# Modulation sums by 32x32 transposes and one fold; the second norm's squares added on VectorE

## The chip, the cores and the metric

The kernel runs on one core of one Trainium2 chip. The metric is the device time of one execution in microseconds (us); less is better. The engines are called TensorE (PE; its weight loads are PEld), VectorE (DVE), ScalarE (ACT), GpSimd (POOL) and SyncE (SP, which here only issues DMAs).

## The reference, cut to what matters

One layer of a block over 512 tokens of width 1024, in float32:

```python
c_act = silu(c)                                   # 1024
mod = c_act @ w_ada + b_ada                       # 1024 x 6144: six rows of 1024
shift1, scale1, gate1, shift2, scale2, gate2 = split(mod, 6)
h = rmsnorm(x, norm1_g) * (1 + scale1) + shift1
... projections, sliding-window attention, stick-breaking attention, merge ...
x = x + gate1 * (merged @ w_out)
h2 = rmsnorm(x, norm2_g) * (1 + scale2) + shift2  # needs sum of x*x over the 1024 features
x = x + gate2 * peer(h2, ...)
out = rmsnorm(x, final_g)
```

Two sums matter here. The modulation row `mod` is a sum over 1024 rows of `w_ada`; its first 16 columns of 128 values are needed before the first projection, the other 32 only after the attention. The second norm needs, for each token, the sum of squares of the new `x` over its 1024 features.

## The kernel before, in words

Features lie on the 128 partitions, tokens on the free axis: `x` is 8 chunks (k) of 128 x 512. Matrix products are made of three TensorE passes on split values (high by high, high by low, low by high; `PASSES`), each a matmul of 128x128 weights against 128x512. A weight block (128x1024) is loaded by SP, its high part is copied by ScalarE (`block_high`, L1010), its low part is subtracted by GpSimd (`block_low`, L562), and TensorE runs its 24 matmuls. Two blocks of split weights are in store, so ScalarE starts on block t + 2 when block t is done. Each engine runs its own program in the order of the code; semaphores order the engines against each other.

The modulation. `w_ada` comes in 12 pieces of 512 columns. `ada_product` (L1344, L1346) on VectorE makes, in 8 instructions over 128x512 in SBUF, each waiting for the one before, a 128x512 partial sum `adap` of a piece: its columns still have to be summed over the 128 partitions. `ada_sum` (L643) does that on TensorE: four float32 matmuls with 128 columns of `adap` as weights and one column of ones as the moving side; each float32 matmul shows as two in the trace, so a sum is 8 rows of 128x1. Pieces 0 to 3 are worked before the attention. Pieces 4 to 11 are worked in the eight heads of the attention loop, one in each.

The attention loop goes over heads n = 0 to 7, two heads to a pair. In each head TensorE runs `heads_scores` (L710 to L725), three or four projection blocks of `FILL[n]` (L684) and, ahead of the third, `turn_probs` (L733) and `later_sums` (the 128x1 rows of L643 for n > 0, then L749, L752), then `head_outputs` (L765, L773). Even heads have value and gate blocks; heads 1, 3 and 5 have the next pair's query and key blocks; head 7 has three gate blocks. VectorE goes in each head through the softmax of the window (L1435 to L1444), the stick-breaking terms (L1450, L1453), `keep(0)` (L1431: a copy of a gate block out of PSUM), `ada_product`, `keep(1)`, then in heads 1, 3 and 5 `rope` (L1408 to L1412), then the other `keep`s and the copies of the outputs (L1462, L1464). `rope` reads bank 7, which `head_outputs` overwrites, so TensorE's L765 waits for `rope_ready`. A projection block writes the bank of the block two before it, so in even heads the fourth block waits for `keep(1)`.

After the loop come eight `up` blocks and eight `out` blocks (L843). After each `out` block m VectorE adds to `x` (L1489), ScalarE squares chunk m into one of two buffers (`squares`, L993), and TensorE sums the squares of chunk m - 1 over the partitions after its block m (`rms_sum`, L630, 8 rows of 128x1). At m = 2 and 4 ScalarE also copies the high part of a query weight (L1112, 128x2048) and GpSimd makes its low part (`query_low`, L567), ahead of its next `block_low`. At the end: the sum of chunk 7, the root on ScalarE (L998), its reciprocal on VectorE, the spread over the partitions on TensorE (L637) and the second norm (L1499).

Of the kernel before, what the change touches and what calls it, by code (L numbers as in the profile page):

```python
# [23 lines left out]
HEADS = 8  # L24
# [36 lines left out]
ALU = mybir.AluOpType  # L61
# [7 lines left out]

(K_ID, K_ONE, K_NTRI, K_NONE, K_SBM, K_CAUS, K_ROT, K_IOTA, K_NEVER, K_SWA, K_INV, K_EPS, K_END) = (  # L70
    0, 128, 256, 384, 512, 640, 768, 896, 1024, 1152, 1408, 1409, 1410)

# [98 lines left out]
def build(nc, xT, small, consts, pos, w_ada, w_blocks, w_qry, skT, euT, ev, eu, gf_row, out):  # L171
    with ExitStack() as ctx:
# [124 lines left out]
        assert att_end <= ARENA - 2 * PAIRS * T, att_end  # L297
        squares2 = yB[:, 2:4, :]

# [63 lines left out]
        def a_buffer(i):  # L363
# [10 lines left out]
        ring_free = [sem(f"ring_free{s}") for s in range(4)]  # L374
        ada_ready, ada_summed, ada_direct, ada_row, ada_turned = map(sem, (
            "ada_ready", "ada_summed", "ada_direct", "ada_row", "ada_turned"))
        hi_ready, h_split, u_hi, u_split, v_hi, v_split, a_split = map(sem, (
# [246 lines left out]
        def _(pe):  # L624
# [14 lines left out]
            def ada_sum(n, b, bank, col):  # L639

                pe.wait_ge(ada_ready, n + 1)
                for m in range(4):
                    last = pe.matmul(bank[:, bass.ds(col + m, 1)], adap[:, b, m * P:(m + 1) * P], ones[:, 0:1], start=(n < 3 and m == 0), stop=True, skip_group_check=True)  # L643
                last.then_inc(ada_summed, 1)
# [5 lines left out]
            for k in range(DC):  # L650
# [3 lines left out]
                last = pe.matmul(ps[4][0:1, :], cact[:, k:k + 1], ring[:, 0, k * 512:(k + 1) * 512], start=(k == 0), stop=(k == DC - 1))  # L654
            last.then_inc(ada_direct, 1)
# [3 lines left out]
            last.then_inc(ada_turned, 1)  # L659
            ada_sum(2, 0, ps[6], 12)  # L660
# [155 lines left out]

            ada_sum(HEADS + 2, 0, ps[2], 256 + 4 * (HEADS - 1))
            pe.wait_ge(oa_out, HEADS)
# [3 lines left out]
            for t in range(UNIT0, len(BLOCKS)):  # L822
# [157 lines left out]
        def _(sa):  # L980
# [3 lines left out]
            def squares(first, dst, chunks=range(DC)):  # L984
                for k in chunks:
                    if k == DC - 1:
                        act_(tiny[:], cst[:, K_EPS:K_EPS + 1], ACT.Sqrt)
                    if first:
                        sa.wait_ge(x_ready, first - DC + k + 1)
                    buffers = dst.shape[1]  # L990
                    if k >= buffers:
                        sa.wait_ge(sq_summed, first + k - buffers + 1)
                    act_(dst[:, k % buffers, :], x[:, k, :], ACT.Square).then_inc(sq_ready, 1)  # L993

            def root(n):

                sa.wait_ge(sq_summed, n * DC)
                act_(rms[:], ps[7][:, 0:TT], ACT.Sqrt, scale=1.0 / D, bias=cst[:, K_EPS:K_EPS + 1]).then_inc(root_ready, 1)  # L998
# [47 lines left out]
            block_high(1)  # L1046
            sa.wait_ge(ada_direct, 1)
            act_(arow[0:1, :], ps[4][0:1, :], ACT.Copy).then_inc(ada_row, 1)
# [82 lines left out]
            for t in range(UNIT0, len(BLOCKS)):  # L1131
# [192 lines left out]
        def _(ve):  # L1324
# [13 lines left out]
            def ada_product(n, slot, b, loads):  # L1338

                ve.wait_ge(ring_in[slot], loads * 16)  # L1340
                if n >= 2:
                    ve.wait_ge(ada_summed, n - 1)
                w = ring[:, slot, :].rearrange("p (k n) -> p k n", k=DC)
# [5 lines left out]
                ins.then_inc(ada_ready, 1)  # L1349
                ve.wait_ge(ada_ready, n + 1)  # L1350
                ve.sem_inc(ring_free[slot], 1)


# [67 lines left out]
            for n in range(HEADS):  # L1421
# [327 lines left out]
def constants():  # L1749
# [80 lines left out]
```

## Time and profile before

| | |
|---|---|
| median of 3 runs | 1722.92 us (1720.43 to 1722.98) |
| span of the profiled execution | 1720.5 us |
| TensorE matmul busy | 1687.4 us, 98% of the span |
| VectorE busy | 1357.2 us, 79% |
| ScalarE busy | 717.8 us, 42% |
| GpSimd busy | 642.7 us, 37% |
| chain that ended last | PE 82%, DVE 15%, issue 2%, ACT 1%, DMA 1% |

The span is from the first to the last instruction of one execution; the profile gives no other time for that execution, and the runs are timed apart from it. In a timeline a row is a start and a length in us from the span's start, then engine, line and operation; the bracket is the time the engine had sat idle, and what ended that. PEclk is TensorE's granted clock, 1.00 for 2.4 GHz and 0.50 for 1.2 GHz. A wait for "issue" is one for which the profile shows no releaser. The attention loop lies at about 84 to 350 us, the `up` blocks to 398, the `out` blocks to 448, the second norm and the first query block to 468; two thirds of the span are the expert stage after them.

### The profile page before, as it was taken

To read this page: it belongs to the slowest core of one execution; us is meant where nothing else is said; L and a number is where in the kernel's file an instruction comes from. 1 tells how busy PE (TensorE), PEld (TensorE's weight loads), DVE (VectorE), ACT (ScalarE), POOL (GpSimd) and SP (SyncE) were. 2 spreads that over 40 slices of the span, in tenths; PEclk is the share of its full clock that TensorE was granted. 3 is DMA by queue.
4 is the path that set the end of the run, shared out by engine and by line. 5 is a ranking of instruction groups with operands and counts; after the bars stand their busy time and mean duration, and the time that the engine had idled before them with its cause. 6 is when DMAs were issued, how large, how long until landed. Compare 5 with 4: busy or idle time off the path is not lost.

```text
span 1720.5 us, 24258 instructions
## 1 busy us (share of the span) xinstructions
PE 1687.4 (98%) x8795; PEld 1490.7 (87%) x8795; DVE 1357.2 (79%) x2770; ACT 717.8 (42%) x1119; POOL 642.7 (37%) x372
## 2 busy tenths in 40 slices
PE   6999999999999999999999999999999999999998
PEld 4688777878899999999999999999999988888886
DVE  7447546674589998999999488888878799989897
ACT  3356455543443443444444333333333344333334
POOL 0322222235356674611111055555434454333331
PEclk9999999999999999999999999999999999999999
DMA  8222332433143433567777899999988899999993
GB/s 338 102 98 86 126 156 86 147 119 139 39 138 115 148 126 102 196 213 286 282 267 266 298 373 362 333 355 339 337 315 307 274 386 407 398 386 384 380 385 123
DMA packets 162156, 417.97 MB, mean 243 GB/s; under 512 B 13584, under 2 KB 83216, under 8 KB 156176
## 3 DMA queue, kind: packets, MB, share of 16 engines
q1 hardware_dynamic: 113680, 266.88, 42.8%
q0 software_dynamic: 36864, 134.23, 21.3%
q10 hardware_dynamic: 11520, 15.73, 2.5%
q8 instruction: 46, 0.75, 0.2%
q14 instruction: 46, 0.38, 0.1%
HBM read 373.80 MB, written 42.99 MB: 242 GB/s over the span
## 4 chain that ended last, share of the span: by engine, by line
PE 82%; DVE 15%; issue 2%; ACT 1%; DMA 1%; POOL 0%; SPq 0%; ACTq 0%
PE bank L944 30%; PE bank L897 22%; PE bank L684 10%; PE bank L843 5%; PE bank L932 5%; PE bank L630 1%; PE bank L710 1%; DVE arena L1595 1%; DVE idx L1534 1%; DVE arena L1556 1%; DVE arena L1548 1%; PE bank L773 1%; DVE arena L1549 1%; DVE slots L1527 1%; PE bank L752 1%
## 5 line engine op out<-in xcount | busy, mean ns | idle before, releaser
L897 PE MATMUL bank<-h_split,u_split 128*128 128x384 f32 x3072 | 556.9, 337 | 2.3 <-DVE u_split L1511 2.0
L897 PEld LDWEIGHTS bank<-h_split,u_split 128*128 128x128 f32 x3072 | 534.6, 188 | 8.6 <-DVE u_split L1511 2.3
L944 PE MATMUL bank<-v_late,a_late 128*128 128x512 f32 x1440 | 326.7, 390 | 0.0
L944 PEld LDWEIGHTS bank<-v_late,a_late 128*128 128x128 f32 x1440 | 270.3, 188 | 56.0
L589 POOL DMA_INDIRECT rows<-eu,idx x128 | 181.3, 1416 | 361.3 <-DVE dots L1516 339.4
L589 POOL DMA_INDIRECT rows<-ev,idx x128 | 173.4, 1355 | 244.3 <-DVE row_sum L1622 211.8
L562 POOL TENSOR_TENSOR block_split<-arena,block_split 128x1024 fp32r<-128x1024 f32 x48 | 117.2, 2445 | 310.5 <-ACT block_split L1010 310.5
L1159 ACT ACTIVATE gelus<-bank 128x384 f32<-128x384 f32 x128 | 62.9, 491 | 370.1 <-PE bank L897 370.0
L944 PE MATMUL bank<-v_split,a_split 128*128 128x512 f32 x864 | 205.4, 391 | 0.0
L944 PEld LDWEIGHTS bank<-v_split,a_split 128*128 128x128 f32 x864 | 161.6, 188 | 31.9
L1622 DVE SCALAR_TENSOR_TENSOR row_sum<-rows,agate,row_sum 128x1024 f32<-128x1024 f32 x127 | 162.6, 1280 | 4.4 <-DVE row_sum L1622 0.5
L684 PE MATMUL bank<-h_hi_part,block_split 128*128 128x512 f32 x512 | 160.9, 396 | 0.5 <-POOL block_split L562 0.5
L1516 DVE CUSTOM_DVE_ANT_0 rows<-rows,h_rows 128x1024 f32<-128x1024 f32 x128 | 151.3, 1220 | 4.4 <-DMA rows<-eu,idx 4.4
L1259 ACT ACTIVATE v_late<-v_raw 128x1024 fp32r<-128x1024 f32 x80 | 84.8, 1060 | 149.8 <-PE bank L944 149.7
L1511 DVE TENSOR_TENSOR u_split<-u_raw,u_split 128x1024 fp32r<-128x1024 f32 x92 | 114.5, 1245 | 39.8 <-ACT u_split L1150 39.8
L1150 ACT ACTIVATE u_split<-u_raw 128x1024 fp32r<-128x1024 f32 x128 | 134.4, 1051 | 0.0
L572 POOL TENSOR_TENSOR u_split<-u_raw,u_split 128x1024 fp32r<-128x1024 f32 x36 | 87.9, 2450 | 109.1 <-ACT u_split L1150 109.1
L1652 DVE TENSOR_TENSOR v_late<-v_raw,v_late 128x1024 fp32r<-128x1024 f32 x80 | 97.8, 1222 | 24.0 <-ACT v_late L1259 22.0
L684 PEld LDWEIGHTS bank<-h_hi_part,block_split 128*128 128x128 f32 x512 | 95.4, 188 | 21.4 <-POOL block_split L562 1.3
L1664 DVE TENSOR_TENSOR weights<-gelus,gates 128x384 f32<-128x384 f32 x128 | 70.9, 554 | 52.0 <-issue 46.3
L1633 DVE TENSOR_SCALAR hot_j<-cst,slots_turned 128x128 f32<-128x128 f32 x384 | 106.5, 344 | 0.0
L1010 ACT ACTIVATE block_split<-arena 128x1024 fp32r<-128x1024 f32 x50 | 52.8, 1056 | 116.3 <-DMA arena<-w_blocks 56.2
(251 smaller groups left out, 2397.3 us busy)
## 6 DMA issues: line engine op xcount, KB each, us to landing
u_raw<-euT SPq DMA_DIRECT2D x128, 512.0 KB, 6.7
v_raw<-ev SPq DMA_DIRECT2D x128, 512.0 KB, 6.8
arena<-w_blocks SPq DMA_DIRECT2D x50, 512.0 KB, 8.9
arena<-w_ada SPq DMA_DIRECT2D x12, 2048.0 KB, 8.1
gates_scratch<-stage SPq DMA_DIRECT2D x24, 1024.0 KB, 10.7
gates<-gates_scratch SPq DMA_DIRECT2D x64, 384.0 KB, 8.1
gelu_scratch<-gelus ACTq DMA_DIRECT2D x80, 192.0 KB, 3.6
gelus<-gelu_scratch SPq DMA_DIRECT2D x80, 192.0 KB, 8.7
```

Source lines behind the costliest of these rows:

```text
L562: nc.gpsimd.tensor_tensor(ws[:, t % 2, 1, :], wraw[:, t % 4, :], ws[:, t % 2, 0, :].bitcast(F32), ALU.subtract).then_inc(w_split, 1)
L572: nc.gpsimd.tensor_tensor(us[:, c % 2, 1, :], ut[:, c % RING, :], us[:, c % 2, 0, :].bitcast(F32), ALU.subtract).then_inc(u_split, 1)
L589: pool.indirect_dma_start(rows[g % NG], None, eu if g < P else ev_rows, bass.IndirectOffsetOnAxis(ap=idx[:, g % P:g % P + 1], axis=0)).the ...
L684: last = pe.matmul(ps[bank][:], ws[:, t % 2, wp, k * P:(k + 1) * P], h1s[xp][:, k, :], start=(k == 0 and q == 0), stop=(k == DC - 1 and q ...
L897: last = pe.matmul(ps[6 + b][:, 0:TD], us[:, b, wp, k * P:(k + 1) * P], hs[:, xp, k, 0:TD], start=(k == 0 and q == 0), stop=(k == DC - 1 a ...
L944: last = pe.matmul(ps[2 * t + f][:], a[:, ap, t * P:(t + 1) * P], v[:, vp, f * 512:(f + 1) * 512], start=(first and q == 0), stop=True, sk ...
L1150: act_(us[:, c % 2, 0, :], ut[:, c % RING, :], ACT.Copy).then_inc(u_hi, 1)
L1511: nv.tensor_tensor(us[:, c % 2, 1, :], ut[:, c % RING, :], us[:, c % 2, 0, :].bitcast(F32), ALU.subtract).then_inc(u_split, 1)
L1516: nv.tensor_tensor_reduce(rows[k % NG], rows[k % NG], hT, 1.0, 0.0, ALU.mult, ALU.add, dots[:, k:k + 1]).then_inc(rows_used, 1)
L1622: nv.scalar_tensor_tensor(acc, rows[g % NG], agate[:, k:k + 1], acc, ALU.mult, ALU.add).then_inc(rows_used, 1)
L1633: ins = nv.tensor_scalar(ohj[:, b, q, :], cst[:, K_IOTA:K_IOTA + P], slotsT[:, 1, t:t + 1], slotsT[:, 2, t:t + 1], ALU.is_equal, ALU.mult)
L1652: nv.tensor_tensor(v_buffer(i)[:, 1, :], vt[:, i % RING, :], v_buffer(i)[:, 0, :].bitcast(F32), ALU.subtract).then_inc(v_split, 1)
```

## The change

1. In the heads, `ada_sum` is gone. After `keep(1)` VectorE runs `ada_fold(n)`: a transpose of `adap` in blocks of 32x32 (128x512), and a reduction of each block's rows to 128x16 values, kept in `ada_parts` (in the space of `dots`).
2. After the last head TensorE sums what is left over the four groups of 32 partitions: 4 float32 matmuls with 32 moving columns and a constant 0/1 matrix `K_FOLD`.
3. `ada_product` always writes `adap[:, 0]`, and no longer waits for sums on TensorE in the heads.
4. In the `out` stage square 0 goes to `square_sum`, squares 1 to 7 to one buffer `square`. VectorE adds squares 1 to 6 to `square_sum`, the one of chunk m - 1 after its L1489 of block m. ScalarE waits for that addition before square m (m >= 2). TensorE has no sum between the blocks; after the last it sums `square_sum` (after addition 6), then `square` (after square 7).
5. The constants lose an unused 128 columns and gain 224: 1410 columns become 1506.

```diff
@@ TensorE
 def later_sums(n):
-                if n:
-                    ada_sum(n + 2, n % 2, ps[2], 252 + 4 * n)
@@ after the heads
-            ada_sum(HEADS + 2, 0, ps[2], 256 + 4 * (HEADS - 1))
+            pe.wait_ge(ada_ready, 3 + 2 * HEADS)
+            of_32 = ada_parts.rearrange("p n (m b) -> p n m b", m=4)
+            for b in range(4):
+                last = pe.matmul(ps[2][:, 256:288].rearrange("p (n m) -> p n m", n=HEADS), cst[:, K_FOLD + 96 - 32 * b:K_FOLD + 224 - 32 * b],
+                                 of_32[:, :, :, b], start=False, stop=True, skip_group_check=True)
+            last.then_inc(ada_summed, 1)
@@ up and out blocks
-                if kind == "out" and m:
-                    rms_sum(DC, squares2, [m - 1])
-            rms_sum(DC, squares2, [DC - 1])
+            pe.wait_ge(squares_added, DC - 2)
+            for t in range(TT):
+                pe.matmul(ps[7][:, t:t + 1], square_sum[:, t * P:(t + 1) * P], ones[:, 0:1], start=(t == 0), stop=False, skip_group_check=True)
+            pe.wait_ge(sq_ready, 2 * DC)
+            for t in range(TT):
+                last = pe.matmul(ps[7][:, t:t + 1], square[:, t * P:(t + 1) * P], ones[:, 0:1], start=False, stop=True, skip_group_check=True)
+            last.then_inc(sq_summed, 1)
@@ ScalarE, out block m
-                    squares(DC, squares2, [m])
+                    if m == DC - 1:
+                        act_(tiny[:], cst[:, K_EPS:K_EPS + 1], ACT.Sqrt)
+                    sa.wait_ge(x_ready, m + 1)
+                    if m >= 2:
+                        sa.wait_ge(squares_added, m - 1)
+                    act_(square if m else square_sum, x[:, m, :], ACT.Square).then_inc(sq_ready, 1)
@@ VectorE
+            def ada_fold(n):
+                step(nv.transpose(adap[:, 1, :], adap[:, 0, :]))
+                nv.tensor_reduce(ada_parts[:, n, :], adap[:, 1, :].rearrange("p (c r) -> p c r", c=16), AX.X, ALU.add).then_inc(ada_ready, 1)
@@ VectorE, head n
                 keep(0)
-                ada_product(n + 3, 0, (n + 1) % 2, n + 2)
+                ada_product(n + 3, 0, 0, n + 2)
                 keep(1)
+                ada_fold(n)
                 if a == 1 and i + 1 < PAIRS:
                     rope(i + 3, halves)
@@ VectorE, out block m
+            def add_square(m):
+                ve.wait_ge(sq_ready, DC + m + 1)
+                if m >= 2:
+                    ve.wait_ge(squares_added, m - 1)
+                nv.tensor_tensor(square_sum, square_sum, square, ALU.add).then_inc(squares_added, 1)
                     nv.scalar_tensor_tensor(x[:, m, :], ps[m % 2][:], part(2, m), x[:, m, :], ALU.mult, ALU.add).then_inc(x_ready, 1)
+                    if m >= 2:
+                        add_square(m - 1)
```

## Rows read from the trace of the kernel before

**Rows 1.** The page: busy time by engine; the chain by engine.
```profile
PE 1687.4 (98%) x8795; PEld 1490.7 (87%) x8795; DVE 1357.2 (79%) x2770; ACT 717.8 (42%) x1119; POOL 642.7 (37%) x372
PE 82%; DVE 15%; issue 2%; ACT 1%; DMA 1%; POOL 0%; SPq 0%; ACTq 0%
```
**Rows 2.** TensorE's waits: who waited for whom, total, times, longest.
```profile
PE bank L765 <- issue: 2.2, 3, 0.7
```
**Rows 3.** Timeline of TensorE in head 1.
```profile
137.66 0.95 PE L643 MATMUL bank<-cst,arena 128*128 128x1 f32 x8
138.48 0.48 PE L752 MATMUL bank<-sp_hi,from_r 128*128 128x512 f32 x1
...
147.67 1.71 PE L765 MATMUL bank<-arena 128*64 128x128 f32 x14 [0.72 <-issue]
```
**Rows 4.** Timeline of VectorE in head 1.
```profile
134.42 9.48 DVE L1346 SCALAR_TENSOR_TENSOR arena<-arena,cact 128x512 f32<-128x512 f32 x7
144.05 1.39 DVE L1408 TENSOR_TENSOR arena<-arena 64x512 f32<-64x512 f32 x2
...
146.18 1.39 DVE L1412 TENSOR_TENSOR arena<-arena 64x512 f32<-64x512 f32 x2
```
**Rows 5.** Timeline of GpSimd, heads 1 and 2.
```profile
154.78 2.38 POOL L562 TENSOR_TENSOR block_split<-arena,block_split 128x1024 fp32r<-128x1024 f32 x1 [13.79 <-ACT block_split L1010]
```
**Rows 6.** Groups by line: busy us, mean ns of one, idle before.
```profile
L1435 DVE TENSOR_REDUCE arena<-bank 128x2 f32<-128x512 f32 x16 | 10.3, 686 | 45.6 <-PE bank L725 45.6
```
**Rows 7.** Timelines of head 6: end of `later_sums`, and `keep(1)`.
```profile
304.96 0.39 PE L749 MATMUL bank<-arena,cst 128*128 128x128 f32 x2
...
309.14 0.69 DVE L1431 COPY arena<-bank 128x512 f32<-128x512 f32 x1
```
**Rows 8.** The clock: a stall of TensorE, and stretches with PEclk ahead of DMA.
```profile
713.65 6.01 PE L897 MATMUL bank<-h_split,u_split 128*128 128x384 f32 x24 [2.01 <-DVE u_split L1511]
...
715.00:716.00 1.00, 1.00 (x4) 1.00 (x4) 1.00 (x2) 0.00 (x0) 0.83 (x2) 0.50 0.77 279
...
148.00:150.00 2.00, 2.00 (x15) 1.49 (x14) 0.58 (x1) 0.00 (x0) 0.00 (x0) 1.00 0.98 414
...
352.00:356.00 4.00, 3.96 (x11) 3.17 (x12) 4.00 (x7) 3.98 (x7) 0.00 (x0) 0.63 0.05 18
```
**Rows 9.** Timeline of TensorE at the end of the `out` blocks.
```profile
449.35 1.05 PE L630 MATMUL bank<-cst,arena 128*128 128x1 f32 x8 [0.72 <-ACT arena L993]
...
451.88 1.97 PE L637 MATMUL bank<-rstd,cst 128*128 128x512 f32 x2 [0.55 <-DVE rstd L1335]
```
**Rows 10.** Timeline of VectorE in the `out` blocks 0, 1, 3, 4, 7.
```profile
404.09 0.75 DVE L1489 SCALAR_TENSOR_TENSOR x<-bank,mod,x 128x512 f32<-128x512 f32 x1 [1.06 <-PE bank L843]
409.53 0.75 DVE L1489 SCALAR_TENSOR_TENSOR x<-bank,mod,x 128x512 f32<-128x512 f32 x1 [4.69 <-PE bank L843]
...
422.31 0.75 DVE L1489 SCALAR_TENSOR_TENSOR x<-bank,mod,x 128x512 f32<-128x512 f32 x1 [5.64 <-PE bank L843]
428.71 0.75 DVE L1489 SCALAR_TENSOR_TENSOR x<-bank,mod,x 128x512 f32<-128x512 f32 x1 [5.64 <-PE bank L843]
...
447.89 0.75 DVE L1489 SCALAR_TENSOR_TENSOR x<-bank,mod,x 128x512 f32<-128x512 f32 x1 [5.64 <-PE bank L843]
```
**Rows 11.** Timelines of ScalarE and GpSimd after `out` block 2.
```profile
417.46 1.90 ACT L1112 ACTIVATE query_hi<-query_raw 128x2048 fp32r<-128x2048 f32 x1
...
419.48 4.60 POOL L567 TENSOR_TENSOR query_lo<-query_raw,query_hi 128x2048 fp32r<-128x2048 f32 x1
424.04 2.40 POOL L562 TENSOR_TENSOR block_split<-arena,block_split 128x1024 fp32r<-128x1024 f32 x1
```
**Rows 12.** GpSimd and VectorE side by side at `up` block 7.
```profile
398.69 2.40 POOL L562 TENSOR_TENSOR block_split<-arena,block_split 128x1024 fp32r<-128x1024 f32 x1 [3.04 <-ACT block_split L1010]
...
398.81 2.83 DVE L1485 TENSOR_TENSOR arena<-arena 128x512 f32<-128x512 f32 x1
```
**Rows 13.** DMA issues: KB, median us to landing.
```profile
cst<-consts SPq DMA_DIRECT2D x1, 705.0 KB, 4.2
```

More of the change, by code:

```diff
@@ L67 @@
 AX = mybir.AxisListType
-(K_ID, K_ONE, K_NTRI, K_NONE, K_SBM, K_CAUS, K_ROT, K_IOTA, K_NEVER, K_SWA, K_INV, K_EPS, K_END) = (
-    0, 128, 256, 384, 512, 640, 768, 896, 1024, 1152, 1408, 1409, 1410)
+(K_ID, K_ONE, K_NTRI, K_NONE, K_SBM, K_ROT, K_IOTA, K_NEVER, K_SWA, K_INV, K_EPS, K_FOLD, K_END) = (
+    0, 128, 256, 384, 512, 640, 768, 896, 1024, 1280, 1281, 1282, 1506)
 S_C, S_G1, S_G2, S_GF, S_B, S_SINK, S_END = 0, 8, 16, 24, 32, 80, 88
@@ L197, in build @@
         agate = sb("agate", [P, P])
+        ada_parts = dots[:].rearrange("p (n c) -> p n c", n=HEADS)
         tsum = sb("tsum", [P, TT])
@@ L297, in build @@
         assert att_end <= ARENA - 2 * PAIRS * T, att_end
-        squares2 = yB[:, 2:4, :]
+        square_sum, square = yB[:, 2, :], yB[:, 3, :]
         top[0] = 0
@@ L374, in build @@
         ring_free = [sem(f"ring_free{s}") for s in range(4)]
-        ada_ready, ada_summed, ada_direct, ada_row, ada_turned = map(sem, (
-            "ada_ready", "ada_summed", "ada_direct", "ada_row", "ada_turned"))
+        ada_ready, ada_summed, ada_row_done, ada_row, squares_added = map(sem, (
+            "ada_ready", "ada_summed", "ada_row_done", "ada_row", "squares_added"))
         hi_ready, h_split, u_hi, u_split, v_hi, v_split, a_split = map(sem, (
@@ L642, in ada_sum @@
                 for m in range(4):
-                    last = pe.matmul(bank[:, bass.ds(col + m, 1)], adap[:, b, m * P:(m + 1) * P], ones[:, 0:1], start=(n < 3 and m == 0), stop=True, skip_group_check=True)
+                    last = pe.matmul(bank[:, bass.ds(col + m, 1)], adap[:, b, m * P:(m + 1) * P], ones[:, 0:1], start=(m == 0), stop=True, skip_group_check=True)
                 last.then_inc(ada_summed, 1)
@@ L654, in _ @@
                 last = pe.matmul(ps[4][0:1, :], cact[:, k:k + 1], ring[:, 0, k * 512:(k + 1) * 512], start=(k == 0), stop=(k == DC - 1))
-            last.then_inc(ada_direct, 1)
+            last.then_inc(ada_row_done, 1)
             pe.wait_ge(ada_row, 1)
@@ L658, in _ @@
                 last = pe.matmul(ps[6][:, 8 + m:9 + m], arow[0:1, m * P:(m + 1) * P], ones[0:1, 0:1], start=True, stop=True, skip_group_check=True)
-            last.then_inc(ada_turned, 1)
+            last.then_inc(ada_row_done, 1)
             ada_sum(2, 0, ps[6], 12)
@@ L987, in squares @@
                         act_(tiny[:], cst[:, K_EPS:K_EPS + 1], ACT.Sqrt)
-                    if first:
-                        sa.wait_ge(x_ready, first - DC + k + 1)
                     buffers = dst.shape[1]
@@ L995, in root @@
             def root(n):
-                sa.wait_ge(sq_summed, n * DC)
+                sa.wait_ge(sq_summed, DC + n - 1)
                 act_(rms[:], ps[7][:, 0:TT], ACT.Sqrt, scale=1.0 / D, bias=cst[:, K_EPS:K_EPS + 1]).then_inc(root_ready, 1)
@@ L1046, in _ @@
             block_high(1)
-            sa.wait_ge(ada_direct, 1)
+            sa.wait_ge(ada_row_done, 1)
             act_(arow[0:1, :], ps[4][0:1, :], ACT.Copy).then_inc(ada_row, 1)
@@ L1340, in ada_product @@
                 ve.wait_ge(ring_in[slot], loads * 16)
-                if n >= 2:
-                    ve.wait_ge(ada_summed, n - 1)
+                if n == 2:
+                    ve.wait_ge(ada_summed, 1)
+                if n == 3:
+                    ve.wait_ge(ada_summed, 3)
                 w = ring[:, slot, :].rearrange("p (k n) -> p k n", k=DC)
@@ L1349, in ada_product @@
                 ins.then_inc(ada_ready, 1)
-                ve.wait_ge(ada_ready, n + 1)
+                ve.wait_ge(ada_ready, n + 1 if n < 3 else 2 * n - 2)
                 ve.sem_inc(ring_free[slot], 1)
+            def ada_fold(n):
+                step(nv.transpose(adap[:, 1, :], adap[:, 0, :]))
+                nv.tensor_reduce(ada_parts[:, n, :], adap[:, 1, :].rearrange("p (c r) -> p c r", c=16), AX.X, ALU.add).then_inc(ada_ready, 1)
             ve.wait_ge(smalls_in, 48)
@@ L1388, in _ @@
             first_low(1)
-            ve.wait_ge(ada_direct, 1)
+            ve.wait_ge(ada_row_done, 1)
             ve.sem_inc(ring_free[0], 1)
             ve.wait_ge(ada_summed, 3)
-            ve.wait_ge(ada_turned, 1)
+            ve.wait_ge(ada_row_done, 2)
             step(nv.tensor_tensor(mod[:, 0:16], ps[6][:, 0:16], sml[:, S_B:S_B + 16], ALU.add))
@@ L1464, in _ @@
                 nv.tensor_copy(yB[lo:hi, i, :], ps[OB_BANK[n]][lo:hi, :]).then_inc(ob_out, 1)
-            ve.wait_ge(ada_summed, 11)
+            ve.wait_ge(ada_summed, 4)
             step(nv.tensor_tensor(mod[:, 16:48], ps[2][:, 256:288], sml[:, S_B + 16:S_B + 48], ALU.add))
@@ L1773, in constants @@
     k[:, K_EPS] = EPS
+    s = np.arange(32)
+    for a in range(4):
+        k[32 * a + s, K_FOLD + 96 + s] = 1.0
     return k
```

1 line of the change is left out of this document (removed).

## The prediction

> **What bounds the kernel now.** I began with the page. TensorE is busy 98% of the span and holds 82% of the chain that ended last, VectorE 15% [rows 1], so each microsecond taken off TensorE counts, unless a stretch hangs on VectorE. The waits of TensorE show such a place: L765, `head_outputs`, stalls three times, 2.2 us in all, with no releaser named [rows 2]. The timelines name it. In head 1 `rope` begins 0.15 us after `ada_product` (134.42 + 9.48 = 143.90), its last instructions end at 146.18 + 1.39 = 147.57, and L765 starts at 147.67, 0.10 us later [rows 3, 4]. The three stalls are of one size, 2.2 in all and 0.7 the longest, and only heads 1, 3 and 5 have a `rope`. L765 needs the bank that `rope` reads. So heads 1, 3 and 5 are set by VectorE from the end of the window scores to the end of `rope`; the other heads, and the `up` and `out` blocks, are set by TensorE.
>
> **Sums taken out of the heads.** A sum costs TensorE 138.48 - 137.66 = 0.82 us [rows 3]. Seven go: in heads 2, 4, 6 and 7 this is 4 x 0.82 = 3.28 us off the path. In heads 1, 3 and 5 it is nothing, since TensorE only comes earlier to L765. Even heads have a second limit close by. In head 6 `later_sums` ends about 305.10, so the fourth block starts one block (5.44 us, the distance of 404.09 and 409.53 [rows 10]) later, at 310.54; `keep(1)`, which frees its bank, ends at 309.83 [rows 7]. The slack is 0.71 us, less than 0.82, and with some 0.05 for the semaphore 0.15 us is given back in heads 2, 4 and 6: 0.45. Head 0 had no sum. The sum after head 7 becomes a fold of as many matmuls, between the same waits; 32 columns in place of one I take at nothing, and up to 0.2 us.
>
> **The fold on VectorE.** No row shows a 32x32 transpose. The nearest for the size is the reduction of 128x512, 686 ns [rows 6]; the reduction to 16 columns reads as much. With the wait between them the pair is 0.72 + 0.66 = 1.38 us. The lower bound is 0.9, if the transpose ran at twice that rate; the upper 2.1, twice the time of the reduction for the transpose. I take the middle value, since both read one float32 operand of 512 columns. GpSimd is idle from 141.0 to 154.78 in head 1 [rows 5], so nothing blocks the pair there. By "VectorE: DVE Perf Modes" of the Trainium skill (The three transpose paths) a 128x128 bfloat16 transpose takes 311 ns, and four of those would be 1.24 us as an upper estimate, making the pair 1.9 us and the sum of the three heads 1.6 us more; no row before shows one. In even heads the pair follows `keep(1)`, which ends at 309.83 in head 6, while the third block runs until 310.54: 0.7 us of it is covered by that wait, and the rest makes the copy of that block late, which nobody needs before the end of the fourth block, 5.44 us on. So it costs nothing; without that cover it would cost the 0.7 us a head. Head 7 has the same distances, and its last copy is needed only after `head_outputs`. In heads 1, 3 and 5 it stands ahead of `rope`, and TensorE, ScalarE's next scores and everything behind L765 wait for it: 3 x 1.38 = +4.14 us (2.7 to 6.3). Its stall at L765 grows from 0.72 to 0.72 + 0.82 + 1.38 = 2.92 us.
>
> **What that stall may do to the clock.** After a stall of 2.01 us at 713.65 TensorE's granted clock fell: 0.50 at 715 to 716 [rows 8], for a time that this row alone does not bound. After today's 0.72 us at L765 it stays at 1.00 [rows 8]. In 352 to 356, where the first `up` block starts, it was 0.63 on average, a loss of 4 x 0.37 = 1.5 us of full clock [rows 8]; that is my price of a fall. A stall of 2.92 us is longer than the 2.01. I expect a fall in most of the three heads; part of each lies in the stall itself or on small matmuls, so I take 1.1 us each, +3.3 us (0 to 4.5).
>
> **Sums taken out of the `out` blocks.** The step from block to block is 5.44 us without a sum (404.09 to 409.53) and 6.40 with one (422.31 to 428.71) [rows 10]: 0.95 us a sum. The sums after blocks 1 to 6 are on the path, 5.7 us; the one after block 7 lies in the wait for the last square.
>
> **What takes a part of it back: GpSimd.** After block 2 ScalarE copies the query's high part (417.46), GpSimd makes the low part (419.48 to 424.08) and only then the low part of block 5's weights, done at 426.44 [rows 11]. TensorE needs that at about 428.5, 0.2 before the x of block 4 [rows 10]. With two sums gone it comes 1.90 us earlier: slack 0.15. But square 2 now waits for the addition of square 1, so the query parts start some 0.7 us later. Moreover an addition can hold GpSimd up by its own 0.69 us, and be held up by it: L1485, also an addition of two SBUF tensors, took 2.83 us when it started inside a GpSimd instruction of 2.40 us [rows 12]. So block 5 stalls 0.55 to 1.25 us, and the pattern repeats after block 4 for block 7. Both together: 1.1 to 2.5, I take +1.4, since the second begins from blocks already spread out. Here "SBUF — State Buffer" of the Trainium skill (Practical consequences) speaks against this change: a VectorE instruction with two SBUF inputs contends with a GpSimd one that reads SBUF, and one of them waits for the whole instruction. The 2.83 us agrees. By that rule alone additions 2 and 4, which begin inside `query_low`, would each wait it out, which is the mechanism already worked out.
>
> **The tail.** Before: x of block 7 ends at 448.64, square 7 is made, TensorE starts its sum at 449.35 [rows 9, 10]. After: addition 6 stands between x and square 7 (+0.72), and TensorE has `square_sum` to sum first, from about the time ScalarE starts square 7. Addition 6 ends at about 448.67 + 0.69 = 449.36, the first sum runs from 449.42 for 0.92, and the second starts at 450.34 where the only one started at 449.35: +1.0. The thin stretch of TensorE gets longer there; the spread's two rows of 512 columns took 1.97 us [rows 9] where 24 such rows of a block take 5.44, so the clock was low there already, and it may now stay so longer: +0.3 (0 to 1.7).
>
> **The constants** grow by 96 of 1410 columns; 705 KB landed in 4.2 us [rows 13], so 48 KB are 0 to 0.3 us, +0.15, at the start, where VectorE waits for the inputs.
>
> The longer waits queue nothing more than is named: behind ScalarE's new wait for an addition stand the query's high part and the weights of the block after next, behind VectorE's additions the next x, which comes 4 us later.
>
> **The sum.** Heads: -3.28 + 0.45 + 4.14 + 3.3 = +4.6. `out` blocks and tail: -5.7 + 1.4 + 1.0 + 0.3 = -3.0. Constants +0.15. Together +1.7 us. Against the profiled span of 1720.5 this is 1722.2; the median of the runs lies 2.4 above that span, for what lies around it and for scatter, so 1722.9 + 1.7 = 1724.6 us.
>
> **The rivals.**
> (a) The clock holds in heads 1, 3 and 5: -1.6 us, 1721.3. For it: the profile has a stall of 0.72 us at this very place without a fall, and TensorE is dense to either side. Against it: the 2.01 us case, which fell.
> (b) Slower: the transpose is dear. It takes twice the reduction's time, 1.38 us in place of 0.69, and the same place, ahead of `rope`, decides: each 0.1 us in it is 0.3 us of time. With the clock falling at the full 1.5 us in all three heads the sum is 1.7 + 2.1 + 1.2 = +5.0 us, 1727.9. It passes 1726.4, slower by 0.2%, from a pair of 2.0 us on at 1.1 us a fall. For it: no row has the operation. Against it: it reads one operand of the same size.
> (c) The change does what it seems to say: VectorE has room, and every sum removed counts: -5.7 (seven at 0.82) - 5.7 + 1.0 = -10.4 us, 1712.5. It needs the pair to be hidden, and L765 to wait for something else than `rope`. The 0.10 us, and stalls in these three heads alone, are against it. In between, a cheap transpose (0.9 us the pair) and no fall give -3.0 us, 1719.9, and with smaller stalls behind GpSimd (0.4 in all) 1718.9.
>
> **How the numbers follow.** Forecast with falls 0.50; (a) 0.22; (b) 0.15; (c) 0.03, the cheap pair without falls 0.10. The range takes in (a), the bounds of the clock term and most of (b): 1719.5 to 1728. A measurement here tells about 0.2% from no change, 3.4 us. Faster by more: (c) and a good part of the cheap pair, 0.11. Slower by more (over 1726.4): (b) and the upper edge of the forecast, 0.20. Within: 0.69.
>
> **What would show it.** In heads 1, 3 and 5 a transpose and a reduction of some 0.7 us each ahead of `rope`, L765 0.1 us behind its end, a stall of 2.9 us, and PEclk of 0.50 in the 4 us after. Head 1 from one L765 to the next longer, head 2 unchanged or shorter. In the `out` stage steps of 5.44 us but for blocks 5 and 7, additions 2 and 4 of over 2 us, and two sums in a row before the root. I am wrong if L765 starts well after `rope`, if PEclk stays 1.00 there, or if GpSimd lets additions through.

## The result and the profile after

The kernel after takes 1729.23 us in the median of 7 runs (1723.97 to 1730.61), the kernel before 1721.89 us (7 runs, 1720.43 to 1722.98): ratio 1.0036, 95% interval 1.0026 to 1.0046. The change makes the kernel slower by 0.36%. The prediction was 1724.6 us with an upper end of 1728.0. It added +1.7 us to 1722.9, the median of three runs; the seven runs of before put that median 1.0 us lower, so the shift that was measured is 7.3 us between the medians and 7.9 between the two profiles.

| | before | after |
|---|---|---|
| span of the profiled execution | 1720.5 us | 1728.4 us |
| TensorE matmul busy | 1687.4 us, 98% | 1685.5 us, 98% |
| VectorE busy | 1357.2 us, 79% | 1372.3 us, 79% |
| mean granted clock of TensorE | 0.994 | 0.989 |

TensorE's row has 104 matmuls fewer and is busy nearly as long. Its list of waits in after (line, who was waited for, total, times, longest) answers to [rows 2]; L765 has become L764, and L952 belongs to the last part of the expert stage:

```profile
PE bank L764 <- issue: 8.8, 3, 2.9
...
PE bank L952 <- DVE a_late L1699: 1.8, 2, 1.4
```

The timeline of VectorE in head 1 of after answers to [rows 4]. The pair, L1368 and L1369, stands between the product and `rope`:

```profile
135.26 9.47 DVE L1359 SCALAR_TENSOR_TENSOR arena<-arena,cact 128x512 f32<-128x512 f32 x7
144.88 0.71 DVE L1368 STREAM_TRANSPOSE arena<-arena 128x512 f32<-128x512 f32 x1
145.63 0.69 DVE L1369 TENSOR_REDUCE dots<-arena 128x16 f32<-128x512 f32 x1
146.23 1.38 DVE L1426 TENSOR_TENSOR arena<-arena 64x512 f32<-64x512 f32 x2
...
148.35 1.38 DVE L1430 TENSOR_TENSOR arena<-arena 64x512 f32<-64x512 f32 x2
```

`rope` ends at 148.35 + 1.38 = 149.73. TensorE in the same head, which answers to [rows 3]:

```profile
149.83 3.22 PE L764 MATMUL bank<-arena 128*64 128x128 f32 x14 [2.94 <-issue]
```

The stall is 2.94 us, and the 14 matmuls behind it take 3.22 us where they took 1.71. The clock says why. Five stretches of after, answering to [rows 8] (the seventh entry after the time is PEclk, then the DMA share):

```profile
147.00:149.30 2.30, 0.00 (x0) 0.00 (x0) 2.24 (x4) 0.53 (x1) 0.00 (x0) 1.00 0.98 406
149.50:152.50 3.00, 2.67 (x13) 2.70 (x14) 0.23 (x1) 0.00 (x0) 0.00 (x0) 0.52 0.95 396
217.70:224.40 6.70, 5.55 (x18) 3.92 (x19) 1.73 (x3) 1.05 (x1) 0.00 (x0) 0.51 0.98 407
289.50:292.50 3.00, 3.00 (x14) 2.59 (x13) 0.40 (x1) 0.00 (x0) 0.00 (x0) 0.51 0.92 382
453.20:459.90 6.70, 6.70 (x28) 5.49 (x28) 1.63 (x6) 1.66 (x4) 0.00 (x0) 0.51 0.01 2
```

All three heads with a stall of 2.9 us fall to 1.2 GHz, at the end of the stall: at 149.3 the clock was still 1.00. Head 3 stays low for twice as long as heads 1 and 5. A new wait is there as well, L952's for `a_late`, 1.8 us in all, at about 1700 us.

**Where the 7.9 us of the two profiles are.** In each head the first reduction of two score columns on VectorE is a mark that both kernels have (L1435 before, L1453 after). Before, heads 1, 2 and 3:

```profile
125.22 1.29 DVE L1435 TENSOR_REDUCE arena<-bank 128x2 f32<-128x512 f32 x2 [4.61 <-PE bank L725]
156.47 1.29 DVE L1435 TENSOR_REDUCE arena<-bank 128x2 f32<-128x512 f32 x2 [4.21 <-PE bank L725]
191.94 1.29 DVE L1435 TENSOR_REDUCE arena<-bank 128x2 f32<-128x512 f32 x2 [4.61 <-PE bank L725]
```

After, heads 1 to 4:

```profile
126.06 1.29 DVE L1453 TENSOR_REDUCE arena<-bank 128x2 f32<-128x512 f32 x2 [4.61 <-PE bank L726]
160.19 1.29 DVE L1453 TENSOR_REDUCE arena<-bank 128x2 f32<-128x512 f32 x2 [4.21 <-PE bank L726]
195.09 1.29 DVE L1453 TENSOR_REDUCE arena<-bank 128x2 f32<-128x512 f32 x2 [4.61 <-PE bank L726]
230.53 1.29 DVE L1453 TENSOR_REDUCE arena<-bank 128x2 f32<-128x512 f32 x2 [4.20 <-PE bank L726]
```

Head 1 took 156.47 - 125.22 = 31.25 us and takes 34.13 now: +2.88. Head 3 takes 35.44, +4.19; head 5 is +3.0 by the same marks. Head 2 went from 35.47 to 34.90: -0.57, and heads 4 and 6 are -0.60 and -0.59. The start, up to head 1, is +0.84. These make head 7's mark 9.14 us late, and the first x of the `out` stage is 8.24 late (below), so head 7 and the `up` blocks give 0.90.

The x rows of the `out` stage answer to [rows 10], with VectorE's additions (L1501) among them. These are blocks 0, 2 to 5 and 7:

```profile
412.33 0.75 DVE L1515 SCALAR_TENSOR_TENSOR x<-bank,mod,x 128x512 f32<-128x512 f32 x1 [1.05 <-PE bank L847]
...
423.24 0.75 DVE L1515 SCALAR_TENSOR_TENSOR x<-bank,mod,x 128x512 f32<-128x512 f32 x1 [4.69 <-PE bank L847]
423.91 0.68 DVE L1501 TENSOR_TENSOR arena<-arena 128x512 f32<-128x512 f32 x1
428.68 0.75 DVE L1515 SCALAR_TENSOR_TENSOR x<-bank,mod,x 128x512 f32<-128x512 f32 x1 [4.09 <-PE bank L847]
429.35 3.01 DVE L1501 TENSOR_TENSOR arena<-arena 128x512 f32<-128x512 f32 x1
434.12 0.75 DVE L1515 SCALAR_TENSOR_TENSOR x<-bank,mod,x 128x512 f32<-128x512 f32 x1 [1.76 <-PE bank L847]
434.79 0.68 DVE L1501 TENSOR_TENSOR arena<-arena 128x512 f32<-128x512 f32 x1
440.43 0.75 DVE L1515 SCALAR_TENSOR_TENSOR x<-bank,mod,x 128x512 f32<-128x512 f32 x1 [4.96 <-PE bank L847]
441.09 2.14 DVE L1501 TENSOR_TENSOR arena<-arena 128x512 f32<-128x512 f32 x1
...
451.33 0.75 DVE L1515 SCALAR_TENSOR_TENSOR x<-bank,mod,x 128x512 f32<-128x512 f32 x1 [4.11 <-PE bank L847]
```

Block 0 is late by 412.33 - 404.09 = 8.24 us, block 7 by 451.33 - 447.89 = 3.44. So the stage gives 4.8 us. Next comes the end of that stage on TensorE, which answers to [rows 9]:

```profile
452.73 1.29 PE L852 MATMUL bank<-cst,arena 128*128 128x1 f32 x8 [1.44 <-DVE arena L1501]
453.88 1.85 PE L855 MATMUL bank<-cst,arena 128*128 128x1 f32 x8
```

and last ScalarE's last `gelus` tile before the expert stage turns to its second half, the first row of before, the second of after:

```profile
1376.77 0.49 ACT L1159 ACTIVATE gelus<-bank 128x384 f32<-128x384 f32 x1 [3.06 <-PE bank L897]
```
```profile
1382.16 0.49 ACT L1170 ACTIVATE gelus<-bank 128x384 f32<-128x384 f32 x1 [3.06 <-PE bank L905]
```

After is 5.4 us late there, and from there to the end of the span it takes 1728.4 - 1382.16 = 346.2 us where before took 343.7. These 2.5 us are in a stage that the change does not touch. Of the rest, heads and start are 8.24, `out` -4.8, and the tail is what the root shows: its reciprocal on VectorE starts at 456.06 for 450.74, 5.32 late, so 1.9 more than block 7. (From there to the last `gelus` tile both kernels take 926.0 to 926.1 us.)

### The profile page after: what moved, and what is told of

It is laid out like the page before. It is cut to its first block, busy times and chain, and to the rows that moved or that the text cites. A ratio compares the mean times of both kernels' runs of the same rounds, so it can differ in the third digit from the quotient of the medians.

```text
span 1728.4 us, 24070 instructions
## 1 busy us (share of the span) xinstructions
PE 1685.5 (98%) x8691; PEld 1485.1 (86%) x8691; DVE 1372.3 (79%) x2792; ACT 719.9 (42%) x1119; POOL 657.9 (38%) x372
## 4 chain that ended last, share of the span: by engine, by line
PE 62%; DVE 20%; DMA 11%; issue 4%; SPq 1%; ACT 1%; POOL 1%; DVEq 0%; ACTq 0%
PE bank L905 22%; PE bank L952 12%; DMA gelus<-gelu_scratch 10%; PE bank L685 10%; PE bank L940 5%; PE bank L847 4%; DVE row_sum L1650 2%; DVE v_late L1680 1%; PE bank L711 1%; PE bank L772 1%; DVE arena L1623 1%; DVE idx L1562 1%; PE bank L764 1%; DVE arena L1584 1%; DVE arena L1576 1%
## 5 line engine op out<-in xcount | busy, mean ns | idle before, releaser
L952 PE MATMUL bank<-v_late,a_late 128*128 128x512 f32 x1440 | 327.2, 390 | 1.8 <-DVE a_late L1699 1.8
L952 PEld LDWEIGHTS bank<-v_late,a_late 128*128 128x128 f32 x1440 | 270.2, 188 | 58.5 <-DVE v_late L1680 2.6
L590 POOL DMA_INDIRECT rows<-ev,idx x128 | 186.6, 1457 | 237.2 <-DVE row_sum L1650 206.6
L952 PE MATMUL bank<-v_split,a_split 128*128 128x512 f32 x864 | 205.4, 391 | 0.0
L952 PEld LDWEIGHTS bank<-v_split,a_split 128*128 128x128 f32 x864 | 161.6, 188 | 31.9
L1279 ACT ACTIVATE a_late<-weights 128x384 fp32r<-128x384 f32 x80 | 42.1, 526 | 175.0 <-DVE weights L1692 175.0
L685 PE MATMUL bank<-h_lo_part,block_split 128*128 128x512 f32 x256 | 99.9, 390 | 0.0
## 6 DMA issues: line engine op xcount, KB each, us to landing
gelus<-gelu_scratch SPq DMA_DIRECT2D x80, 192.0 KB, 12.3
```

What stands on the lines that cost most here:

```text
L590: pool.indirect_dma_start(rows[g % NG], None, eu if g < P else ev_rows, bass.IndirectOffsetOnAxis(ap=idx[:, g % P:g % P + 1], axis=0)).the ...
L685: last = pe.matmul(ps[bank][:], ws[:, t % 2, wp, k * P:(k + 1) * P], h1s[xp][:, k, :], start=(k == 0 and q == 0), stop=(k == DC - 1 and q ...
L952: last = pe.matmul(ps[2 * t + f][:], a[:, ap, t * P:(t + 1) * P], v[:, vp, f * 512:(f + 1) * 512], start=(first and q == 0), stop=True, sk ...
```

## The experiments

First the parts alone, the pair moved, and the clock by itself. `a_mod_only` is after with the squares' part undone, `b_sq_only` is before with the squares' part done and the constants of after. Each ratio is to runs of the kernel before from the same time; small differences between kernels are read from the ratios, since the median of before itself moved between 1721.76 and 1722.37 us.

> The changed kernel with the squares of the second norm put back as before: the modulation part alone. Theory 1 (the pair ahead of rope lengthens heads 1, 3 and 5, and the stall of 2.9 us that it leaves on TensorE lets the clock fall): 4.1 - 2.8 for the sums removed, +5 to 7 us of clock in three falls, +6 to +8 us against the kernel before. Rival 2 (the pair costs its own time only, the falls are hidden in waits): +1.3 us. Rival 3 (the loss is in the squares part, in the contention with GpSimd): at most +1.3 us here.

> The changed kernel with the modulation sums put back on TensorE as before: the squares part alone. Theory 1: the out blocks gain 4.8 us, the tail gives 1.0 us back by the second sum and 1 us by the clock, so -2.5 to -3 us against the kernel before, and no stall over 0.8 us at head_outputs. Rival 3: slower than before by 3 us or more.

Measured: a 1729.51 us, ratio 1.0049 (1.0035 to 1.0063); b 1723.03 us, 1.0003 (0.9993 to 1.0012). The loss is with the modulation part: a is 7.4 us slower in the medians, within the 6 to 8 of theory 1. But b gained nothing where 2.5 to 3 us were expected, although the last `gelus` tile came 5.5 us earlier than before (1371.24 for 1376.77): between that tile and the end of the span it lost 5.2 us. Something that both carry costs time late in the kernel.

`c_fold_late` leaves all work in place and moves the pair behind `rope`:

```diff
                 keep(1)
-                ada_fold(n)
                 if a == 1 and i + 1 < PAIRS:
                     rope(i + 3, halves)
+                ada_fold(n)
```

> The changed kernel with the transpose and the reduction behind rope instead of ahead of it. Theory 1: the stall at head_outputs shrinks from 2.94 to 1.55 us, 4.1 us of time go directly and the clock falls in fewer of the three heads or in none, another 2 to 6 us: -6 to -10 us against the changed kernel, so 0 to -3 us against the kernel before. Rival 2 (no cost of the clock): -4.1 us against the changed kernel.

`d_fill` is after, the pair where it was, with 11 matmuls of 128x512 into a bank that nobody reads at that time, ahead of L764 in heads 1, 3 and 5:

```diff
+                if a == 1 and i + 1 < PAIRS:
+                    pe.wait_ge(probT_ready, n + 1)
+                    for k in range(11):
+                        pe.matmul(ps[4][:], ident_r, h1s[0][:, k % DC, :], start=True, stop=True)
```

> The changed kernel with 11 matmuls of 128x512 that nobody reads put ahead of head_outputs in heads 1, 3 and 5, in the stall that TensorE has there (2.5 of its 2.94 us). It adds work and takes no wait away. Theory 1: the granted clock stays at 1.00 in these heads and the time falls by 4 to 6 us against the changed kernel. Rival 2: no difference, or up to 0.5 us slower. The heads should still be 1.38 us longer by the pair.

Measured: c 1718.47 us, 0.9981 (0.9972 to 0.9990); d 1722.35 us, 1.0002 (0.9993 to 1.0011). Both came about as theory 1 had them. The fill takes no work away, it adds 33 matmuls, and it is 1.0036 - 1.0002 = 0.34% faster than after, 5.9 us. Head 1 of d on TensorE, and its clock over the same time:

```profile
146.70 2.74 PE L815 MATMUL bank<-h_hi_part,ident_r 128*128 128x512 f32 x11
149.80 1.71 PE L764 MATMUL bank<-arena 128*64 128x128 f32 x14 [0.36 <-issue]
```
```profile
146.00:150.00 4.00, 3.64 (x17) 2.68 (x16) 3.62 (x6) 0.60 (x1) 0.00 (x0) 1.00 0.74 305
150.00:154.00 4.00, 4.00 (x23) 2.55 (x22) 0.99 (x2) 0.00 (x0) 0.00 (x0) 1.00 0.98 401
```

L764 starts within 0.03 us of where it did in after: the wait for `rope` is the same. Only the clock differs, and the 14 matmuls take 1.71 us again. The marks of d for heads 1 and 2:

```profile
126.02 1.29 DVE L1457 TENSOR_REDUCE arena<-bank 128x2 f32<-128x512 f32 x2 [4.61 <-PE bank L726]
158.60 1.29 DVE L1457 TENSOR_REDUCE arena<-bank 128x2 f32<-128x512 f32 x2 [4.21 <-PE bank L726]
```

That is 32.58 us, 1.33 more than before; heads 3 and 5 give 32.57 and 32.58. So the pair costs 1.33 us a head, and what after has above it is the clock: 2.88 - 1.33 = 1.55, 4.19 - 1.33 = 2.86 and 3.0 - 1.33 = 1.7, 6.1 us in all. The marks of d are 6.1 us ahead of those of after from head 7 on. In c the stall is as long as the removed sum makes it, and no fall follows in the heads:

```profile
147.88 1.71 PE L764 MATMUL bank<-arena 128*64 128x128 f32 x14 [1.59 <-issue]
```

Next the late loss. All four kernels and after lost time behind the last `gelus` tile. The constants' tile had grown by 96 columns, which pushes every tile behind it in SBUF by 384 bytes. `e_pad_only` is before with that growth alone, `f_aligned` is after with 32 columns more, 512 bytes from before, and `i_pad_64` is before with 64 columns, 256 bytes. The columns hold zeros and are loaded with the rest:

```diff
 e_pad_only, from before
-    0, 128, 256, 384, 512, 640, 768, 896, 1024, 1152, 1408, 1409, 1410)
+    0, 128, 256, 384, 512, 640, 768, 896, 1024, 1152, 1408, 1409, 1506)
 i_pad_64, from before: 1474 in its place
 f_aligned, from after
-    0, 128, 256, 384, 512, 640, 768, 896, 1024, 1280, 1281, 1282, 1506)
+    0, 128, 256, 384, 512, 640, 768, 896, 1024, 1280, 1281, 1282, 1538)
```

> The kernel before with 96 empty columns behind its constants, nothing else: all later tiles of SBUF lie 384 bytes higher, as in the changed kernel, and the constants take 48 KB more to load. In all five changed kernels seen so far the last stage of the expert values, where the DMA queues are full, lost 2.4 to 3.6 us against the kernel before, while everything up to it was shifted by one constant. Theory 4 (the place of the tiles costs the loss): +2.5 to +3.5 us, all of it after 1380 us in the trace. Rival 5 (it comes from the changed order of work): 0 to +0.3 us.

> The changed kernel with 32 more empty columns behind its constants, so that all later tiles lie 512 bytes above those of the kernel before, at the same place modulo 512. Theory 4: 2.5 to 3.5 us faster than the changed kernel. Rival 5: no difference.

> The kernel before with 64 empty columns behind its constants: all later tiles 256 bytes higher. If the loss of the kernel with 96 empty columns (+3.4 to 4.1 us) comes from tiles that do not start at a multiple of 256 bytes from where they did, this one loses nothing: 0 to +0.3 us. If any shift, or one other than 512 bytes, costs: +3 us.

Measured: e 1725.90 us, 1.0020 (1.0011 to 1.0029); f 1725.99 us, 1.0022 (1.0013 to 1.0031); i 1722.15 us, 0.9999 (0.9990 to 1.0008). Columns that nobody reads cost 3.4 us, 32 more of them take 2.4 us off after, and 64 cost nothing. The first and the third are what theory 4 and the expectation had; f gained a little less than the 2.5 to 3.5 us. So it is neither the load nor the size, but the place. Waits from 1380 us on, TensorE's and VectorE's in e, then VectorE's in i:

```profile
PE bank L944 <- DVE a_late L1671: 1.9, 1, 1.9
```
```profile
DVE weights L1664 <- issue: 32.8, 24, 2.5
```
```profile
DVE v_late L1652 <- ACT v_late L1259: 23.3, 32, 0.9
DVE weights L1664 <- issue: 1.9, 2, 1.2
```

L1671 makes `a_late` from what L1664 writes. The six kernels with the tiles 384 bytes off have this wait of TensorE, 1.8 to 2.9 us at about 1700 us, and none of the other eight has it. In b and e the clock fell there as well, a loss of 1.7 us. L1664 reads the `gelus` that come back from HBM; the profile names no releaser, but their loads landed later. The rows of the DMA issues (KB each, median us from issue to landing), of before, after, e, f and i:

```profile
gelus<-gelu_scratch SPq DMA_DIRECT2D x80, 192.0 KB, 8.7
```
```profile
gelus<-gelu_scratch SPq DMA_DIRECT2D x80, 192.0 KB, 12.3
```
```profile
gelus<-gelu_scratch SPq DMA_DIRECT2D x80, 192.0 KB, 12.4
```
```profile
gelus<-gelu_scratch SPq DMA_DIRECT2D x80, 192.0 KB, 8.6
```
```profile
gelus<-gelu_scratch SPq DMA_DIRECT2D x80, 192.0 KB, 8.3
```

The loads of `v_raw` (512 KB) did the same, 6.8 us in before and 9.5 to 9.8 in after and e. The time from the last `gelus` tile to the end of the span parts the kernels with no exception: 343.7 to 343.8 us in those at 0, 256 or 512 bytes from before (before, f to l), 346.2 to 349.0 us in the six at 384 (after, a to e). For e this is 3.9 us; its last `gelus` tile comes 1.4 us earlier than that of before, since two falls of the clock that before has, at 353 and 715 us, are missing in its profile (1.6 and 1.2 us by the marks, against a start that is 1.4 late).

With the tiles 512 bytes off, the parts can be told apart again. `g_fold_late_aligned` is c and `j_sq_aligned` is b, each with 32 columns more.

> The pair behind rope, with the same 32 empty columns. Theory 4: 2.5 to 3.5 us faster than the pair behind rope alone (1718.5), so about 1715.5. Rival 5: 1718.5.

> The squares part alone, with the tiles 512 bytes above those of the kernel before. Theory 4: 2.5 to 3 us faster than the squares part alone without it, so -2.5 to -3.5 us against the kernel before, which is what the out blocks gain (4.8) less the tail (1.5 to 2). Rival 5: no difference to the kernel before.

Measured: g 1716.48 us, 0.9970 (0.9958 to 0.9982); j 1718.93 us, 0.9980 (0.9971 to 0.9989). The squares' part alone is worth 0.20%, 3.4 us, as expected. The fold behind `rope` seems to add to that: 0.10%, 1.7 us, but the intervals overlap. The marks bear it out: from head 1's to head 7's g takes 197.98 us and j 199.78. Against c, g is 0.11% faster, 1.9 us, where 2.5 to 3.5 were expected.

Last, what beats both. `h_rope_first` puts `rope` inside the product, ahead of its fourth multiplication, in heads 1, 3 and 5, so that it ends at 143.5 us in head 1, where after ends it at 149.7:

```diff
                 for k in range(1, DC):
+                    if between and k == at:
+                        between()
...
-                ada_product(n + 3, 0, 0, n + 2)
+                turns = a == 1 and i + 1 < PAIRS
+                ada_product(n + 3, 0, 0, n + 2, (lambda: rope(i + 3, halves)) if turns else None, 3)
```

> As the one before, but in heads 1, 3 and 5 rope stands inside the modulation product, after its first three instructions; the pair follows the product. Rope then ends some 4 us earlier, so TensorE should no longer wait at head_outputs in these heads (before: 0.72 us each) and the sums removed there count too: 3 x (0.72 + 0.82) = 4.6 us faster than the pair behind rope, with the clock at 1.00. Rival: the product ends 3.5 us later, frees its buffer later and the next weight blocks arrive too late: no gain.

Measured: 1726.91 us, 1.0036 (1.0022 to 1.0049), 10.4 us slower than g in the medians, from which it differs by the place of `rope` alone; 4.6 us faster was expected. No stall at L764 is left in its waits, and heads 1, 3 and 5 take 29.6 us. But heads 2, 4 and 6 take 39.6, 38.7 and 40.7 us where g has 34.9, 34.9 and 34.5. TensorE and ScalarE wait elsewhere; the last row is g's, where that wait is 19 us less:

```profile
PE bank L685 <- DVE arena L1451: 8.1, 3, 2.7
...
ACT block_split L1016 <- DMA arena<-w_blocks: 76.1, 11, 14.9
```
```profile
ACT block_split L1016 <- DMA arena<-w_blocks: 57.1, 11, 12.5
```

The product ends later (147.43 us in head 1, 144.73 in after), and SP holds the loads of the next weights back with it: `ada_load`, which waits until the product has freed its ring, stands ahead of the `block_load`s of the head. Two kernels turn that order round, `k_fold_late_sp` from g and `l_rope_first_sp` from h:

```diff
-                if n + 5 < 12:
-                    ada_load(n + 5)
                 for k in range(len(FILL[n])):
                     block_load(AT[FILL[n][k]] + 4)
+                if n + 5 < 12:
+                    ada_load(n + 5)
```

> The pair behind rope, tiles aligned, and in the heads SP issues the load of the next piece of the modulation weights after the block loads instead of ahead of them. A control for the next kernel: TensorE does not wait for weight blocks here, so no change against 1716.5, within 0.5 us.

> rope inside the modulation product, with the SP order of the kernel before this one, so that the block loads no longer stand behind a load that waits for the end of the product. If the late blocks made rope first slow, it now gains what was expected: no stall at head_outputs, 3 x (0.72 + 0.82) = 4.6 us off, about 1712. If VectorE's or GpSimd's order is the reason: 1720 or more.

Measured: k 1717.55 us, 0.9971 (0.9960 to 0.9982), the same ratio as g within 0.01%: without a late product that order changes nothing. l 1709.93 us (5 runs, 1708.61 to 1711.49), 0.9930 (0.9916 to 0.9944), the fastest of all, 12.4 us below before. Heads 2, 4 and 6 are back at 34.9, 34.9 and 34.5 us, so it was the order on SP that made h slow. Its wait for the weights' loads is down to one of 3.4 us, and from one mark to the next head 1 takes 29.60 us where before took 31.25:

```profile
125.52 1.29 DVE L1455 TENSOR_REDUCE arena<-bank 128x2 f32<-128x512 f32 x2 [4.61 <-PE bank L726]
...
155.12 1.29 DVE L1455 TENSOR_REDUCE arena<-bank 128x2 f32<-128x512 f32 x2 [4.21 <-PE bank L726]
```

The clock stays at full level where `up` begins (around 350 us) and in the expert stage at about 709 us, where before and g fell. The two profiles are 1720.5 - 1706.9 = 13.6 us apart. Of these the three odd heads are 3 x 1.65 = 4.95 us, heads 2, 4 and 6 are 1.7, head 7 and the `up` blocks 2.5, the `out` stage with its tail 3.9, and the time from the root to the last `gelus` tile 0.9; the start takes 0.3 back. The 2.5 are 1.6 more than the 0.90 of after, so the two missing falls are worth some 2.5 us together. Why the clock stays up at these two places was not tried.

## Why the prediction was wrong, step by step

| term | forecast | profile after |
|---|---|---|
| start, constants | +0.15 | +0.84 |
| the pair, 3 heads | +4.14 | +4.0 (3 x 1.33, from d) |
| clock in the heads | +3.3 (0 to 4.5) | +6.1 |
| sums out of heads 2, 4, 6, 7 | -2.83 | -2.7 (0.57 + 0.60 + 0.59, and 0.90 from head 7 and the `up` blocks) |
| `out` blocks | -4.3 | -4.8 |
| tail | +1.3 | +1.9 |
| after the last `gelus` tile | 0 | +2.5 |
| sum | +1.7 | +7.8 of 7.9 |

**What held.** The place that decides: L764 starts 0.10 us after `rope` ends, as L765 did [rows 3, 4]. Transpose and reduction take 0.71 and 0.69 us and together shift `rope` by 1.38 us at the forecast's digit; the stall is 2.94 us for 2.92. The reduction [rows 6] was the right stand-in for the transpose, and the 1.24 us that the prediction set beside it was too much. Even heads give 0.57 to 0.60 us for a forecast of 0.67. In `out` the steps are 5.44 us, additions 2 and 4 take 3.01 and 2.14 us inside GpSimd's instructions, and block 5 comes 0.87 us late (6.31 for 5.44), within 0.55 to 1.25. The squares' part alone is 3.4 us for 3.0.

**The step that failed: the price of a clock fall.** That the clock falls behind the stall was forecast and came; the term for it was +3.3 us with an upper end of 4.5, and it measured +6.1. The prediction took 1.5 us for a whole fall, from a mean clock of 0.63 over 352 to 356 [rows 8], and took off 0.4 of it, since a part would lie in the stall or on small matmuls. Three things were wrong with that. The stretch ended before the fall did: the next two microseconds of the same trace read

```profile
356.00:358.00 2.00, 2.00 (x9) 1.61 (x8) 0.11 (x1) 1.27 (x3) 0.00 (x0) 0.89 0.00 0
```

so that fall loses 1.5 + 2 x 0.11 = 1.7 us of full clock. Little of it lies in the stall: the clock is at 1.00 until the last half microsecond, and L764's 14 matmuls pay 3.22 - 1.71 = 1.51 us by themselves; heads 1 and 5 paid 1.55 and 1.7 where 1.1 was reckoned. And a fall may last twice as long: head 3 stayed low for 6.7 us and paid 2.86. The trace of before has falls of both lengths, and the prediction read only a short one. At the start of the kernel, behind a wait of 12.8 us, it reads

```profile
42.50:49.00 6.50, 4.41 (x9) 2.50 (x9) 6.12 (x12) 3.69 (x5) 0.00 (x0) 0.50 0.90 378
```

`f_aligned` has its long one in head 1. Which head gets it is not settled by the runs; the seven runs of after lie between 1723.97 us at a clock of 0.992 and 1730.61 at 0.989, while the runs of c, whose profile has no fall in the heads, lie within 3.3 us. That the number and length of the falls make this spread was not tried.

**The step that was missing: the place of the tiles.** The constants were costed as 48 KB of load. That they move every tile behind them was not thought of, and it costs 2.5 us in the profile of after, 3.4 us in the runs of e. By these sizes neither this nor the clock's 2.8 alone would have left the stated range; both together did. Here the Trainium skill, "DMA: Bandwidth & Descriptors" (How a descriptor splits into AXI transactions), had a rule that speaks against the change: an AXI transaction must start at a 256-byte boundary, so a descriptor that does not start on one fetches bytes that it does not use. The page tells this of reads, and the loads here write SBUF, so it bears on them by likeness only. The runs agree in what costs: the program places the tiles that follow (`arena_at`) at byte 27136 of each partition in before, 27392 in i and 27648 in f, all multiples of 256, and at 27520 in after and e, 128 bytes past one. No other misplacement was tried, and no run shows how the loads are cut up. Up to the expert stage the same shift cost nothing that the marks show.

**Smaller.** The tail cost 1.9 us for 1.3. Two sums in a row came as foreseen, but the clock fell at 453.2, so the second took 1.85 us where a sum took 1.05 [rows 9]. In b, c, d, f, g and j, with the same two sums and a later fall, the same stretch is only 0.8 us longer than in before, so 1.0 us of the 1.9 is the clock. The stall of block 7 did not come (445.87 to 451.33, 5.46 us), since GpSimd ended its split for that block at 442.64 + 2.84 = 445.48, before the x of block 6 at 445.87; for block 5 it had ended at 434.60, behind the x of block 4 at 434.12. The start is 0.84 us late; in b and c, with the same constants, head 1's mark moves less (0.23 us in c). Over all the kernels that mark scatters from 0.49 us early (j) to 1.39 late (e), so one profile does not show what the constants cost at the start.

**By the rivals.** (a), the clock holds, is what d and c show for a filled or shorter stall, not for this kernel. (b) named the right place and the right sign but the wrong price: not the transpose, its fall term was what counted, and at 4.5 us that was still 1.6 short. (c) needed L764 to wait for something else than `rope`, and it did not. With the forecast's sum, +1.7, the clock's +2.8 and the placement's +2.5 alone make +7.0.

## What to carry to other kernels

A wait added in front of a dense stretch of TensorE costs its own length and then the slow matmuls behind it; price the second from a row of the same matmuls at either level and from a fall read to its end, allow for one of double length, and see whether the stall can be filled or the work moved behind whoever TensorE waits for. When a change resizes a tile that stands ahead of others in SBUF, keep the shift of the others a multiple of 256 bytes, which cost nothing here, or measure the growth by itself: the cost showed far away, in the last stage, where the DMA engines' busy share is 0.98. Where a producer is moved for the sake of one waiter, look at what else waits behind its end: `rope` moved alone turned a kernel of 1716.5 us into one of 1726.9, and with two statements of SP's order turned round it gave 1709.9.

## What the runs showed of the hardware that I had not expected

- TensorE after a stall: after 1.59 us (c) the clock stayed at 1.00 at this place, after 2.94 us it fell in all three heads of after. With 11 matmuls of 128x512 in that stall, 2.74 us of work whose result nobody uses, it stayed at 1.00 and the kernel was 5.9 us faster.
- The falls read to their end in before, after and f come in two sizes, but for those that the end of the span cuts: 1.7 us of full clock lost (before at 353, 452 and 715, after in heads 1 and 5) or 3.4 (before at 42, after in head 3 and at 453, f in head 1).
- The 14 matmuls of 128x128 take 1.71 us at 2.4 GHz and 3.22 us in the fall, nearly 1.9 times as long.
- A shift of all tiles by 384 bytes lengthened the median landing of a 192 KB load from 8.7 to 12.4 us (12.3 in after, 12.4 in e), and shifts of 256 and 512 bytes left it at 8.3 and 8.6.
- A 32x32-block transpose of 128x512 float32 on VectorE takes 0.71 us, as long as a reduction or an addition of that size.
- An addition of two SBUF tiles of 128x512, 0.68 us alone, took 3.01 us when it started inside a GpSimd instruction of 4.60 us. GpSimd's next split took 2.85 us in place of 2.42:

```profile
427.20 4.60 POOL L568 TENSOR_TENSOR query_lo<-query_raw,query_hi 128x2048 fp32r<-128x2048 f32 x1 [0.34 <-ACT query_hi L1118]
431.75 2.85 POOL L563 TENSOR_TENSOR block_split<-arena,block_split 128x1024 fp32r<-128x1024 f32 x1
```
